# Down products of two of three SwiGLU groups from seven half products, in a float32r decoder step on one Trainium2 core

## The reference

```python
def swiglu(x, wg, wu, wd):
    hid = jax.nn.silu(jnp.einsum('btd,df->btf', x, wg)) * jnp.einsum('btd,df->btf', x, wu)
    return jnp.einsum('btf,fd->btd', hid, wd)
...
    x = layer_norm(ALPHA * x + 0.5 * swiglu(x, ffn1_wg, ffn1_wu, ffn1_wd), ln1_g, ln1_b)
    z = jnp.einsum('btd,de->bte', x, w_in)
    ...   # short causal convolution, pooling branch, gated merge to m
    x = layer_norm(ALPHA * x + jnp.einsum('btd,de->bte', m, w_out), ln2_g, ln2_b)
    x = layer_norm(ALPHA * x + 0.5 * swiglu(x, ffn2_wg, ffn2_wu, ffn2_wd), ln3_g, ln3_b)
```

## Time and profile before

| | us |
|---|---|
| median of 3 runs | 1079.19 (1079.13 to 1080.92) |
| the profiled execution | 1080.36 |
| its span, first to last instruction | 1078.6 |
| PE busy | 1055.5 |
| DVE busy | 637.8 |
| POOL busy | 528.8 |
| ACT busy | 435.7 |

### The profile page before, as it was taken

One profiled execution on the slowest core, in us unless ns is written; L12 is line 12 of the kernel. 1 busy time (PEld: TensorE's weight loads), 2 busy tenths in 40 slices (PEclk: granted clock), 3 DMA queues, 4 the chain that ended last, 5 costly groups with the idle time before them and its releaser, 6 DMA issues.

```text
span 1078.6 us, 20719 instructions
## 1 busy us (share of the span) xinstructions
PE 1055.5 (98%) x8731; PEld 1049.4 (97%) x8731; DVE 637.8 (59%) x911; ACT 435.7 (40%) x658; POOL 528.8 (49%) x311
## 2 busy tenths in 40 slices
PE   7999999999999999999999999999999999999996
PEld 7999999999999999999999999989999999999996
DVE  6988811287745865722524237888774126776476
ACT  4554532155553343332322324455545113545233
POOL 4365654155657254753553555225556424556421
PEclk9999999999999999999999999999999999999998
DMA  8133244234345040542322344102434323333402
GB/s 255 38 103 109 77 110 118 78 99 118 98 137 138 2 123 22 140 118 66 115 86 79 114 115 109 40 21 80 117 99 118 89 74 103 109 109 86 114 26 80
DMA packets 195001, 103.29 MB, mean 96 GB/s; under 512 B 4420, under 2 KB 193428, under 8 KB 194901
## 3 DMA queue, kind: packets, MB, share of 16 engines
q1 hardware_dynamic: 194827, 101.85, 33.3%
q10 hardware_dynamic: 82, 0.12, 0.1%
HBM read 99.74 MB, written 2.48 MB: 95 GB/s over the span
## 4 chain that ended last, share of the span: by engine, by line
PE 89%; DVE 7%; ACT 2%; issue 1%; DMA 1%; POOL 0%; ACTq 0%; DVEq 0%; POOLq 0%
PE ps L1321 14%; PE ps L1318 14%; PE ps L1319 14%; PE ps L1301 14%; PE ps L1303 14%; PE ps L1302 14%; DVE x L1177 1%; DVE xl L939 1%; DVE x L1158 1%; DMA raw<-in_ffn_wd_dram 1%; DVE form_lo L990 1%; PE ps L1364 1%; PE ps L1371 1%; PE ps L1365 1%; PE ps L1424 1%
## 5 line engine op out<-in xcount | busy, mean ns | idle before, releaser
L569 POOL TENSOR_TENSOR wl<-raw,wh 128x512 fp32r<-128x512 f32 x120 | 226.5, 1915 | 219.0 <-DVE raw L965 173.4
L615 ACT ACTIVATE wh<-raw 128x1024 fp32r<-128x1024 f32 (+3 forms) x203 | 238.4, 1178 | 191.4 <-DMA raw<-in_ffn_wd_dram 103.6
L1301 PE MATMUL ps<-form_hi,wh 128*128 128x260 f32 x640 | 182.2, 285 | 4.1 <-ACT temps L615 4.1
L1303 PE MATMUL ps<-form_hi,wl 128*128 128x260 f32 x640 | 181.9, 284 | 0.0
L1302 PE MATMUL ps<-form_lo,wh 128*128 128x260 f32 x640 | 181.7, 284 | 0.0
L1318 PE MATMUL ps<-xh,wh 128*128 128x260 f32 x640 | 167.0, 282 | 0.7 <-ACT yp L615 0.7
L1319 PE MATMUL ps<-xl,wh 128*128 128x260 f32 x640 | 166.5, 282 | 0.0
L561 POOL TENSOR_TENSOR wl<-raw,wh 128x1536 fp32r<-128x1536 f32 (+2 forms) x36 | 107.8, 3006 | 104.3 <-ACT wh L615 104.2
L1318 PE MATMUL ps<-hid_hi,wh 128*128 128x260 f32 x544 | 141.9, 282 | 0.0
L1319 PE MATMUL ps<-hid_lo,wh 128*128 128x260 f32 x544 | 141.9, 283 | 0.0
L1301 PE MATMUL ps<-xh,wh 128*128 128x260 f32 x480 | 136.0, 283 | 0.6 <-POOL wl L569 0.6
(11 more groups left out here) (221 smaller groups left out, 2303.3 us busy)
## 6 DMA issues: line engine op xcount, KB each, us to landing
raw<-in_ffn_wg_dram SPq DMA_DIRECT2D x80, 256.0 KB, 3.3
raw<-in_w_in_dram SPq DMA_DIRECT2D x40, 512.0 KB, 4.0
raw<-in_ffn_wd_dram SPq DMA_DIRECT2D x16, 768.0 KB, 5.0
b<-in_ffn_wu_dram SPq DMA_DIRECT2D x40, 256.0 KB, 3.4
raw<-in_ffn_wu_dram SPq DMA_DIRECT2D x40, 256.0 KB, 3.1
raw<-in_ffn_wd_dram SPq DMA_DIRECT2D x16, 640.0 KB, 5.4
raw<-in_w_out_dram SPq DMA_DIRECT2D x7, 512.0 KB, 3.9
xrow<-in_x_prompt_dram SPq DMA_DIRECT2D x4, 512.0 KB, 6.0
```

The costliest lines, as they stand in the source:

```text
L569: nc.gpsimd.tensor_tensor(wl_slot[:, s, :], raw_slot[:, s, :], wh_slot[:, s, :].bitcast(F32), ALU.subtract).then_inc(lo_ready, 1)
L615: return nc.scalar.activation(out, in_, ACT.Copy)
L1301: mm(out, hi, vh, start=start and n == 1, stop=False, skip_group_check=more)
L1303: ins = mm(out, lo, vh, start=False, stop=n == count, skip_group_check=more)
```

## The change

The 22 hidden blocks are used in three groups, 8, 6 and 8. For the first two the down product is also computed with Winograd's scheme: two output blocks (2j, 2j + 1) by two token halves, contraction split into even and odd hidden blocks of the group. These are four "down units" a group, of seven half products of 4 (group 0) or 3 (group 1) blocks. They run in one row with the up pairs, as 28 units: the down units of group g stand behind the first up unit of group g + 1. The last group keeps plain chunks, of 8 blocks.

- Matmuls: a SwiGLU's down product had (12 + 10) x 8 x 6 = 1056. Now it is 4 x 84 + 4 x 63 + 8 x 8 x 6 = 972.
- For the first two groups DVE makes sums of the hidden values as well (`mid_sums`: `fourth_sum` for an even block, three more for an odd one), ACT rounds them (`round_mid`), DVE makes their rests (`mid_rest`). `xl32` is a new buffer; parts of `xh` and `xl` carry the fourth sum.
- A down unit's results go onto x in six additions of 128x260: those out of PSUM in `down_first`, `down_second`, `down_fourth`, those of the kept products in `down_kept`, one unit later. `down_first` and the others stand for `gate_first`, `up_first` and `up_second` of an up unit. `first_p` and its siblings have one buffer each; ACT's copies wait on `p_taken`, `q_taken`, `u_taken`.
- The sums T1 and T3 are written to PSUM (banks 6 and 7) instead of `raw` from unit 3 on. `weight_sums` loses T4, which is `last_sum` now, behind rest_thirteen; hid_pair stands behind that; rest_twenty_four stands last.
- ACT's order within a unit is new too: copy P1 (behind `round_thirteen`, if the unit before was a down unit), round_thirteen, copy Q5, round the loaded weights, Silu of the second gate, copy P1 + P6, hid_up, round_twenty_four, round_mid, Silu of the first gate.
- Chunks of the last group are split by POOL in two halves. The slots of the ring that chunks use are new.

The diff, cut to its core; removed lines are left out, since the functions before are printed above.

```diff
+    GROUPS = (8, 6, 8)
+    GROUP_AT = [sum(GROUPS[:g]) for g in range(len(GROUPS))]
+    LAST_GROUP = len(GROUPS) - 1
+    assert sum(GROUPS) == KF and LAST_GROUP == 2 and max(GROUPS[:-1]) == 2 * HK and not any(g % 2 for g in GROUPS)
+    UNITS = [None]
+    for g in range(len(GROUPS)):
+        for f in range(max(GROUP_AT[g], 2), GROUP_AT[g] + GROUPS[g]):
+            UNITS.append(("up", f))
+            if g and f == GROUP_AT[g]:
+                UNITS += [("down", g - 1, j) for j in range(K // 2)]
+    NU = len(UNITS) - 1
+    LAST_UP = KF - 1
+    assert NU % 2 == 0 and UNITS[NU] == ("up", LAST_UP)
...
+        def thirteen_whole(n, p):
+            return ps[:, 6:8, 0:kblocks(p) * P] if p > 2 else thirteen(raw_slot, n, p)
...
+                    down = UNITS[p][0] == "down"
+                    def keep(out, in_, sign, taken):
+                        if no > 1:
+                            act.wait_ge(taken, no - 1)
+                        nc.scalar.activation(out, in_, ACT.Copy, scale=sign if down else 1.0).then_inc(kept, 1)
+                    act.wait_ge(w_used, number[n, "P1", p])
+                    if was[0] != "down":
+                        keep(first_p, x_bank, 1.0, p_taken)
+                    if p < NU:
+                        round_thirteen(n, p + 1)
+                    else:
+                        round_chunk((n, "down", 0))
+                    if was[0] == "down":
+                        keep(first_p, x_bank, 1.0, p_taken)
+                    act.wait_ge(w_used, number[n, "Q5", p])
+                    keep(first_q, z_bank, 1.0, q_taken)
+                    if p < NU:
+                        round_unit(n, p + 1)
+                    else:
+                        round_chunk((n, "down", 1))
+                    if was[0] == "up":
+                        second_gate(p - 1)
+                    act.wait_ge(w_used, number[n, "P6", p])
+                    keep(first_u, x_bank, -1.0, u_taken)
+                    if was[0] == "up":
+                        hid_up(was[1], p % 2)
+                    ends = was[0] != "down" and was[1] + 1 in GROUP_AT
+                    if ends:
+                        round_mid(was[1])
+                    if p < NU:
+                        round_twenty_four(n, p + 1)
+                    if was[0] != "down" and not ends:
+                        round_mid(was[1])
+                    if not down:
+                        act.wait_ge(p_taken, no)
+                        nc.scalar.activation(bank((p + 1) % 2, 0), gate_sum, ACT.Silu).then_inc(s.on1, 1)
                 round_form(n, 0)
                 if n == 0:
+                    round_thirteen(n, 1)
                 gate_opened(0)
                 round_form(n, 1)
                 if n == 0:
...
+            def weight_sums(n, p):
+                b11, b22, t2 = (slot[n, name, p] for name in ("B11", "B22", "T2"))
+                no, cols = unit_no(n, p), kblocks(p) * P
                 for name in ("B11", "B22"):
+                    dve.wait_ge(land[slot[n, name, p]], landed[n, name, p])
+                dve.wait_ge(b12_in[p % 2], 16 * (NU // 2 * n + (p + 1) // 2))
+                if p <= 2 and free[n, "T1", p]:
+                    dve.wait_ge(w_used, max(free[n, "T1", p], free[n, "T3", p]))
+                if p == 3:
+                    dve.wait_ge(ffn[n].hid_ready, 2)
+                elif p > 3:
+                    dve.wait_ge(t13_ready, no - 1)
+                whole = thirteen_whole(n, p)
+                tt(whole, slots(raw_slot, slice(b11, b22 + 1, 2), p),
+                   b12[:, p % 2, 0:cols].unsqueeze(1).broadcast_to([P, 2, cols]), ALU.add).then_inc(t13_made, 1)
+                dve.wait_ge(t13_made, no)
+                if free[n, "T2", p]:
+                    dve.wait_ge(w_used, free[n, "T2", p])
+                tt(slots(raw_slot, t2, p), whole[:, 0, :], slots(raw_slot, b22, p), ALU.add).then_inc(t2_made, 1)
+            def last_sum(n, p):
+                b21, t2, t4 = (slot[n, name, p] for name in ("B21", "T2", "T4"))
+                no = unit_no(n, p)
+                dve.wait_ge(t2_made, no)
+                dve.wait_ge(land[b21], landed[n, "B21", p])
+                if free[n, "T4", p]:
+                    dve.wait_ge(w_used, free[n, "T4", p])
+                tt(slots(raw_slot, t4, p), slots(raw_slot, t2, p), slots(raw_slot, b21, p), ALU.add).then_inc(t4_made, 1)
+            def rest_thirteen(n, p):
+                dve.wait_ge(t2_made, unit_no(n, p))
+                dve.wait_ge(t13_round, unit_no(n, p))
+                tt(thirteen(wl_slot, n, p), thirteen_whole(n, p), thirteen(wh_slot, n, p).bitcast(F32),
                    ALU.subtract).then_inc(t13_ready, 1)
+            def rest_twenty_four(n, p):
...
+                def fourth_sum(f, pair):
+                    ins = tt(fourth_whole((f - GROUP_AT[group_of(f)]) // 2), bank(pair, 0), even32[:, 1, :], ALU.subtract)
+                    ins.then_inc(s.mid_made if f in MID_NO else s.mid_step, 1)
+                    if f not in MID_NO:
+                        step.n += 1
+                def mid_sums(f, pair):
+                    i = (f - GROUP_AT[group_of(f)]) // 2
+                    dve.wait_ge(s.hid_round, f + 1)
+                    if f % 2 == 0:
+                        fourth_sum(f, pair)
+                        return
+                    if i:
+                        dve.wait_ge(s.mid_made, MID_NO[f - 1])
+                    else:
+                        dve.wait_ge(s.mid_step, step.n)
+                    first = step.on(stt(mid32[:, 1, i, :], fourth_whole(i), -1.0, bank(pair, 1), ALU.mult, ALU.subtract))
+                    tt(mid32[:, 0, i, :], even32[:, 1, :], bank(pair, 1), ALU.subtract)
+                    dve.wait_ge(s.mid_step, first)
+                    tt(mid32[:, 2, i, :], mid32[:, 1, i, :], bank(pair, 0), ALU.add).then_inc(s.mid_made, 1)
+                def mid_rest(f):
+                    i = (f - GROUP_AT[group_of(f)]) // 2
+                    dve.wait_ge(s.mid_round, MID_NO[f])
+                    if f % 2:
+                        ins = tt(mid_lo[:, :, i, :], mid32[:, :, i, :], mid_hi[:, :, i, :].bitcast(F32), ALU.subtract)
+                    if f % 2 == 0 or i == 0:
+                        ins = tt(half(xl[:, i, :], 1), fourth_whole(i), half(xh[:, i, :], 1).bitcast(F32), ALU.subtract)
...
+                def onto(p, y, product, op=ALU.add):
+                    if UNITS[p][1] == 0:
+                        return stt(y, y, 2.0 * ALPHA, product, ALU.mult, op)
+                    return tt(y, y, product, op)
+                def down_first(p):
+                    j, q, done = UNITS[p][2], (p + 1) % 2, parts_no(p - 1)
+                    if done:
+                        dve.wait_ge(s.part, done)
+                    else:
+                        residual_free(2 * n)
+                    dve.wait_ge(w_used, number[n, "P2", p])
+                    onto(p, half(x32[:, 2 * j, :], 0), bank(q, 0))
+                    dve.wait_ge(w_used, number[n, "Q3", p])
+                    onto(p, half(x32[:, 2 * j + 1, :], 0), bank(2, q)).then_inc(s.part, 1)
+                def down_second(p):
+                    dve.wait_ge(w_used, number[n, "P7", p])
+                    onto(p, half(x32[:, 2 * UNITS[p][2] + 1, :], 1), bank((p + 1) % 2, 1),
+                         ALU.subtract).then_inc(s.part, 1)
+                def down_kept(p):
+                    j, no = UNITS[p][2], unit_no(n, p)
+                    a, b = x32[:, 2 * j, :], x32[:, 2 * j + 1, :]
+                    dve.wait_ge(kept, 3 * no)
+                    dve.wait_ge(s.part, parts_no(p - 1) + 2)
+                    tt(half(a, 0), half(a, 0), first_p, ALU.add).then_inc(p_taken, 1)
+                    tt(half(b, 0), half(b, 0), first_u, ALU.add).then_inc(u_taken, 1)
+                    tt(half(b, 1), half(b, 1), first_q, ALU.add).then_inc(q_taken, 1)
+                def down_fourth(p):
+                    dve.wait_ge(w_used, number[n, "Q4", p])
+                    onto(p, half(x32[:, 2 * UNITS[p][2], :], 1), bank((p + 1) % 2, 1)).then_inc(s.part, 1)
+                def mid_rests(f):
+                    if f - 1 in MID_NO:
+                        mid_rest(f - 1)
...
+                def unit_steps(p):
+                    was, now = UNITS[p - 1] or ("open", 1), UNITS[p]
+                    if was[0] == "up":
+                        up_second(p - 1)
+                    elif was[0] == "down":
+                        down_second(p - 1)
+                    f, pair = (was[1], p % 2 if was[0] == "up" else 3) if was[0] != "down" else (None, None)
+                    if p < NU:
+                        weight_sums(n, p + 1)
+                    if f in MID_NO and f % 2 == 0:
+                        mid_rests(f - 1)
+                    elif was[0] == "down":
+                        down_kept(p - 1)
+                    if p < NU:
+                        rest_thirteen(n, p + 1)
```

(72 more changed lines are left out.)

646 lines of the change are left out of this document (307 added, 339 removed).

## The result

The changed kernel takes 1102.35 us (median, 1101.72 to 1103.04), the kernel before 1079.95: a ratio of 1.0208, with a 95% interval of 1.0194 to 1.0222. The change costs 22.4 us where 15.8 were forecast (1095 against 1079.2). Its profiled span is 1101.2 us, that of before 1078.6.

The account below looks back on a forecast made before the run. PE's stream of matmuls was taken to bound the kernel. 1080.4 (profiled execution) - 20.1 (gain) + 19.6 (kept products) + 16 (DVE's slips) = 1095.9, less 1.2 against the median: 1095 us, range 1071 to 1108.

Parts of the forecast that it names:

- full second cost: Rival: DVE's slips in up units cost all of 24.4 us, giving 1103, up to 1108 with POOL's share; chance 0.20.
- Gain: PE's down product: 84 matmuls fewer per SwiGLU at 0.1197 us each, 10.05 us, twice: 20.1 us saved.
- s = 1.65: Start of DVE's weight sums (line 955), 1.65 us after the unit's P1, bound by the landing of B22's load.
- faster rival: Weight sums not bound by the load, starting from s = 0.85, so group 0's P6 finds its copy: 1068; chance 0.18.
- First cost: PE waits before P6 because ACT's copy of P1 needs first_p freed: 9.8 us a SwiGLU, 19.6 in all.
- Second cost: DVE slips behind in up units of groups 0 and 1: 12.2 us a SwiGLU, 24.4 in full, 16 taken.
- The slip per unit: In up units the start of DVE's weight sums grows by 0.45 us a unit until a stall resets it.
- The opening: Start of a SwiGLU: last_sum stands behind a rest (1.2) and a sum, costing 1.5 us.
- waits at group ends: First down unit's Q4 waits for up_second, 1.4 and 2.0 us; units behind lose 1.55 and 1.2 more.
- two thirds: Share taken of the 24.4 us second cost, since a tenth saved early removes a stall: 16 us.
- At no cost: List priced at nothing: ACT's extra roundings and copies, loads with same bytes per matmul, smaller last chunks, first span's residual additions.
- Kept alone: Rival: only the kept products cost, DVE's spare time absorbs its slips: 1079, 1075 to 1087; chance 0.20.

Follow-up runs that it names:

- split additions: Changed kernel with ACT copying P1 before rounding the sums and DVE adding only first_p's kept product before the weight sums, the other two behind: 1078.83 us, 0.9989.
- 8 columns: Changed kernel with the hidden values' sums, roundings and rests made on 8 columns instead of 260, PE reading other operands of the same shape: 1092.42 us, 1.0110.
- ACT's move alone: Changed kernel with only ACT's order changed, copy of P1 before the rounding of the weight sums, also after down units: 1091.42 us, 1.0107.
- with the slots mended too: Changed kernel with ACT's P1 copy moved ahead, only first_p's addition before the weight sums, and the last ring slots of three lists exchanged: 1075.50 us, 0.9956.
- DVE's move alone: Changed kernel with only DVE's order changed, all kept additions before the weight sums; ACT still rounds before copying P1: 1108.95 us, 1.0267.
- both queues changed: Changed kernel with DVE's kept additions moved before the weight sums and ACT's copy of P1 before their rounding: 1084.34 us, 1.0036.

## Why the prediction was right or wrong

The sign and the mechanism of the largest loss were right; the sum fell 7 us short. The measured 1102.35 lies in the stated range (1071 to 1108), but above the forecast's own band (1087 to 1100, chance 0.42) and in that of the full second cost (0.20). That the sum is no further off is in part luck: one term is 8 us too large, one 4 too small, and some 10 us were in no term. The table takes both SwiGLUs together, in us.

| term | predicted | shown | by |
|---|---|---|---|
| matmuls gone | -20.1 | -19.8 | 84 left out of the kernel before |
| kept products | +19.6 (0 to 23) | +24.0 | stretches, changed kernel against split additions |
| DVE's slips, with ACT's roundings | +16 taken, 24.4 full | +8.1 | stretches, changed kernel against 8 columns |
| ring slots | nothing | +2.9 to +3.3 | slots swapped, in two kernels |
| not separated | | about +7.5 | what is left of 22.6 |

**Gain.** Right to 0.3 us. Spacing times count was enough, since the profile before showed PE's stream to be the time.

**Start of the weight sums.** s = 1.65 was right. In the changed kernel the copy of P1 starts at 77.61 and 87.71, so by the same reckoning as in the prediction these units began at 76.17 and 86.27; line 1068 starts at 77.87 and 88.09, s = 1.70 and 1.82. (PE's own timeline puts P1 earlier: by it s was 1.86 before, 63.50 to 65.36, and is 1.97 and 2.03 in these two units.) The faster rival rested on s near 0.85 and falls.

**First cost, 19.6 against 24.** The chain and the list of eight waits were right. Of the sizes in SwiGLU 1, group 1 was predicted as 1.45, 1.45, 2.2, 1.5 and measured, from matmul to matmul, as 1.48, 1.64, 2.52 and 1.74; in group 0 four times 0.8 stand against 1.73, 1.03, 0.93 and 0.88. Two things were left out of the term. The second down unit, the first of the four in group 0, waits 0.7 us longer than its fellows: it stands behind the group's end, and its weight sums start at 130.86, 2.72 us after P1 (128.14) instead of 1.85. The prediction had put this lateness (1.55 us) under the second cost. And the longest waits have an echo. PE in the fourth down unit of group 1:

```profile
257.12 0.56 PE L1518 MATMUL ps<-mid_hi,wh 128*128 128x260 f32 x1 [2.36 <-ACT temps L800]
257.47 0.42 PE L1519 MATMUL ps<-mid_lo,wh 128*128 128x260 f32 x1
257.69 0.42 PE L1520 MATMUL ps<-mid_hi,wl 128*128 128x260 f32 x1
```

The matmuls behind it are 0.22 us apart instead of 0.12 for some 13 of them, about 1.3 us. In SwiGLU 2 the same happens twice, behind P6 of this unit and of the one after it (15 matmuls, 1.5 us each), so the lower clock takes some 4 us; behind the first unit, neither the kernel before nor that with split additions has any of it. The prediction had named this as a possibility and given it no price. The longest wait of all, 3.24 us at 962.69, is in that last unit of SwiGLU 2; its weight sums start 3.88 us after P1, where they start 2.22 after it in SwiGLU 1. Why they are late isn't shown.

The chain had both things that stand in front of the copy right. It took the later one, the rounding, and so it is (144.32 for the end of the addition, 145.10 for that of the rounding); with the rounding out of the way the addition still holds the copy (0.48 us, ACT's move alone).

**Second cost, 16 against 8.** The step on the slip failed first. The slip per unit was put at 0.45 us, from a chain in which rest_twenty_four waits for POOL until s + 8.85 and the next unit's sums start at s + 10.5. DVE in up units of the changed kernel:

```profile
67.64 1.22 DVE L1068 TENSOR_TENSOR ps<-raw,b 128x1024 f32<-128x1024 f32 x1
...
75.06 0.69 DVE L1123 TENSOR_TENSOR two_lo<-ps,two_hi 128x520 fp32r<-128x520 f32 x1
...
76.34 1.27 DVE L1092 TENSOR_TENSOR wl<-raw,wh 128x1024 fp32r<-128x1024 f32 x1
...
77.87 1.22 DVE L1068 TENSOR_TENSOR ps<-raw,b 128x1024 f32<-128x1024 f32 x1
...
85.68 2.15 DVE L1092 TENSOR_TENSOR wl<-raw,wh 128x1024 fp32r<-128x1024 f32 x1
...
88.09 1.22 DVE L1068 TENSOR_TENSOR ps<-raw,b 128x1024 f32<-128x1024 f32 x1
```

Line 1092 takes 1.27 us behind an odd block, where POOL's splits end at 76.53, and 2.15 behind an even one, beside a split. Line 1068 starts every 10.22 us (77.87, 88.09, and on to 98.32 and 108.53), against 10.06 of a unit: the slip is 0.16. The step that failed is the end of the chain: POOL's splits end where they were put (8.89 us after line 1068 at 67.64), but what stands between them and the next sums takes 1.34 us and not 1.65. From matmul to matmul PE loses 0.75 us once to hid_rest, before P1 at 75.90, and then 0.14 to 0.19 every second unit. The opening was put at 1.5 us; the first two units of SwiGLU 1 take 21.78 us against 21.28 before (43.03 to 64.81, and 42.22 to 63.50), 0.5 more. The waits at group ends came where they were expected and smaller: 0.62 us for up_second where 1.4 was said (and 0.48 for the rests of the sums), 0.27 and 0.35 where group 1 was put at 2.0. The second step that failed is the two thirds taken of the full sum, a guess about terms that cancel: it was one third.

**At no cost.** Of this list the loads were wrong. The prediction counted bytes and not slots: the diff moves entries of the ring, and a slot sets when a load may start. In the second norm this put 3.45 us before an instruction of DVE's queue. The smaller last chunks were right: their stretch is shorter by 11.6 us in each SwiGLU, against 96 x 0.1197 = 11.5.

**Rivals.** The full second cost (1103) is nearest by number and wrong by cause: slips of 8 us, not of 24. Kept alone (1079) falls with the 8.1 us and with what no term held: by the table it would have been 1084.

**What stays open.** With the kept products mended, the two SwiGLU stretches are still 7.1 and 7.2 us longer than before, beyond the 12 matmuls. By the kernel with 8 columns 8.1 of these 14.3 us go to the additional work of DVE and ACT; 6.2 do not. With 0.6 us at the start and what the slots leave between the SwiGLUs that is the last line of the table. PE's timeline says in what form they are lost: against the kernel before, stops of 0.1 us and more before a half product grew by 5.5 and 5.9 us, and the matmuls right behind stops, 0.20 us apart instead of 0.12, by about 1.3 and 1.0. Among the stops are the kept copies that still come late in group 1 (0.62 and 0.41 us in SwiGLU 1, 0.60 and 0.39 in SwiGLU 2) and, in this profile alone, 1.8 us in the fifth and sixth unit of SwiGLU 2, where the weight sums start 3.74 us after P1; with the slots mended too, the second stretch is 1.7 us shorter. Which of the other stops are DVE's isn't separated. That the shares add up so is worked out, not tried: no kernel ran with both taken away.

## What to carry to other kernels

When a scheme keeps a result in a single buffer for one more unit, follow that buffer through both in-order queues: what stands in front of the instruction that frees it, and what stands in front of the one that fills it. A saving of matmuls is worth count times spacing only if the helpers' chain of one unit (here 10.22 us against 10.06), and not only their sum of work, stays under the unit. Where a diff changes the slots of a ring, write down for each load which reader frees its slot and what waits behind the load's user.

## What the runs showed of the hardware

A wait can cost more than itself: after the 2.36 us wait at 257.12 matmuls run at near half their rate for some 13 instructions. The granted clock, last number but two of each window of the changed kernel:

```profile
257.00:258.00 1.00, 0.88 (x4) 0.91 (x5) 1.00 (x2) 1.00 (x2) 0.00 (x0) 0.50 0.00 0
258.00:259.00 1.00, 1.00 (x7) 1.00 (x7) 0.96 (x3) 0.63 (x1) 0.23 (x1) 0.50 0.00 0
259.00:260.00 1.00, 1.00 (x6) 1.00 (x6) 0.00 (x0) 0.55 (x2) 1.00 (x1) 0.50 0.00 0
```

0.50 is the level of 1.2 GHz. The fall does not follow each wait of that length. Behind a longer gap, 2.95 us at 135.48 in the kernel with DVE's move alone, and behind one of 2.46 us at 252.59 in the kernel with 8 columns, the clock stayed at the level of 2.4 GHz (one window of each, in this order):

```profile
134.00:140.00 6.00, 4.52 (x37) 4.55 (x38) 2.58 (x4) 4.29 (x6) 2.88 (x3) 1.00 0.01 3
251.00:257.00 6.00, 4.41 (x37) 4.44 (x38) 4.56 (x10) 4.18 (x6) 2.76 (x3) 1.00 0.04 12
```

An addition of DVE with both inputs in SBUF was stretched beside POOL's splits from 0.42 to 1.00 and 1.51 us (the kernel with both queues changed). The prediction had allowed 0.2 us for this. The Trainium skill, "SBUF — State Buffer", section "SBUF: two separate sides", has the two engines lock each other out for a whole instruction; the additional 0.58 and 1.09 us stay under the 1.29 of a split, as that rule wants.
